# Opening of a two-layer backbone step: small loads on ScalarE's queue, first modulation by halves of the contraction, gate products behind chunk one

## What is computed

```python
sh1, sc1, gt1, sh2, sc2, gt2 = split(silu(cond) @ w_mod[l] + b_mod[l], 6)   # w_mod[l]: 1024 x 6144
h    = rmsnorm(x) * g * (1 + sc1) + sh1              # modulation
proj = h @ w_in                                      # 1024 x 3600: 7 chunks of 512 columns, 16 columns a | b
gate = -exp(a_log) * softplus(proj_a + dt_bias)      # DeltaNet decay, from the last 16 columns
beta = sigmoid(proj_b)
# then: 2-D neighbourhood attention | chunked gated DeltaNet -> w_out -> dense SwiGLU
# layer 1: pooling mixer -> top-2-of-8 SwiGLU experts -> final norm
```

## Time and profile before

| | |
|---|---|
| time before, median of 3 runs | 1436.82 us (1436.22 to 1437.96) |
| the profiled execution | 1437.28 us |
| its span in the profile | 1435.6 us (1.7 us lie around it) |
| PE busy | 1362.7 us, 95% of the span |
| DVE, ACT, POOL busy | 326.4, 306.1, 95.1 us |
| mean DMA rate | 348 GB/s |
| chain that ended last | PE 84%, DMA 7%, SP's issuing side 4%, DVE 3%, ACT 2% |

### The profile page before, as it was taken

One profiled execution on the slowest core, in us unless ns is written; L12 is line 12 of the kernel. 1 busy time (PEld: TensorE's weight loads), 2 busy tenths in 40 slices (PEclk: granted clock), 3 DMA queues, 4 the chain that ended last, 5 costly groups with the idle time before them and its releaser, 6 DMA issues.

```text
span 1435.6 us, 28151 instructions
## 1 busy us (share of the span) xinstructions
PE 1362.7 (95%) x12676; PEld 721.0 (50%) x12676; DVE 326.4 (23%) x415; ACT 306.1 (21%) x404; POOL 95.1 (7%) x175
## 2 busy tenths in 40 slices
PE   4999899889999998999999999999999999999976
PEld 1997586768888875343333333333333343343322
DVE  1564544655444445000000000100000000000005
ACT  2557344443443423010000010010000000010002
POOL 5101040320000001000000000000000000000012
PEclk9799999999999999999999999999999999999999
DMA  8755838899565549999999999999999999999994
GB/s 336 272 180 187 345 155 307 327 391 340 183 197 175 191 173 419 399 424 424 420 424 424 398 425 409 395 422 425 398 424 424 399 423 425 397 419 425 420 422 195
DMA packets 125186, 500.24 MB, mean 348 GB/s; under 512 B 10716, under 2 KB 14632, under 8 KB 103568
## 3 DMA queue, kind: packets, MB, share of 16 engines
q1 hardware_dynamic: 110464, 471.98, 82.7%
q10 hardware_dynamic: 12208, 18.12, 3.5%
q0 software_dynamic: 2400, 8.42, 1.4%
HBM read 478.81 MB, written 19.69 MB: 347 GB/s over the span
## 4 chain that ended last, share of the span: by engine, by line
PE 84%; DMA 7%; SPq 4%; DVE 3%; ACT 2%; issue 1%; ACTq 0%; DVEq 0%
PE ps L2197 34%; PE ps L2245 13%; PE ps L413 6%; PE ps L415 6%; PE ps L414 6%; PE ps L1706 4%; DMA raw<-in_moe_down 4%; PE ps L2240 3%; SPq L536 2%; DMA raw<-in_moe_up 2%; PE ps L1720 2%; PE ps L1811 1%; PE ps L1812 1%; PE ps L1813 1%; DMA raw<-in_w_mod 1%; SPq L433 1%
## 5 line engine op out<-in xcount | busy, mean ns | idle before, releaser
L2197 PE MATMUL ps<-raw,hTf 128*32 128x512 f32 (+1 forms) x2128 | 209.4, 545 | 4.0 <-DMA raw<-in_moe_up 3.2
L2197 PE MATMUL ps<-ring_a,hTf 128*32 128x512 f32 (+1 forms) x2096 | 203.0, 538 | 2.1 <-ACT hTf L1120 1.1
L1658 DVE TENSOR_TENSOR hm<-gate_bc,ps 128x384 f32<-128x384 f32 (+1 forms) x30 | 18.2, 607 | 711.2 <-PE ps L2197 710.3
L376 DVE TENSOR_TENSOR w_lo<-raw,w_hi 128x2048 fp32r<-128x2048 f32 x60 | 138.1, 2308 | 139.8 <-ACT w_hi L372 139.7
L2197 PE MATMUL ps<-ring_b,hTf 128*32 128x384 f32 (+1 forms) x1408 | 139.2, 540 | 4.2 <-DMA ring_b<-in_moe_up 2.9
L372 ACT ACTIVATE w_hi<-raw 128x2048 fp32r<-128x2048 f32 x60 | 114.4, 1913 | 118.9 <-PE ps L415 114.1
L2197 PEld LDWEIGHTS ps<-raw,hTf 128*32 128x32 f32 x2128 | 68.2, 110 | 130.8 <-issue 124.3
L2197 PEld LDWEIGHTS ps<-ring_a,hTf 128*32 128x32 f32 x2096 | 67.9, 110 | 122.2 <-issue 117.8
L413 PE MATMUL ps<-w_hi,hTh 128*128 128x512 f32 x272 | 107.3, 394 | 1.5 <-DVE w_lo L376 1.5
L415 PE MATMUL ps<-w_lo,hTh 128*128 128x512 f32 x272 | 106.6, 392 | 0.0
L414 PE MATMUL ps<-w_hi,hTl 128*128 128x512 f32 x272 | 106.4, 391 | 0.0
(11 more groups left out here) (375 smaller groups left out, 1486.3 us busy)
## 6 DMA issues: line engine op xcount, KB each, us to landing
raw<-in_w_mod SPq DMA_DIRECT2D x48, 1024.0 KB, 7.7
raw<-in_moe_down SPq DMA_DIRECT2D x21, 2048.0 KB, 24.5
ring_a<-in_moe_down SPq DMA_DIRECT2D x21, 2048.0 KB, 25.8
raw<-in_moe_up SPq DMA_DIRECT2D x14, 2048.0 KB, 24.7
ring_b<-in_moe_down SPq DMA_DIRECT2D x14, 2048.0 KB, 24.9
ring_a<-in_moe_gate SPq DMA_DIRECT2D x13, 2048.0 KB, 21.3
raw<-in_moe_gate SPq DMA_DIRECT2D x11, 2048.0 KB, 23.3
ring_a<-in_moe_up SPq DMA_DIRECT2D x10, 2048.0 KB, 19.4
```

Source lines behind the costliest of these rows:

```text
L376: nc.vector.tensor_tensor(w_lo[:, w % SPLIT], raw[:, slot % RAW], w_hi[:, w % SPLIT].bitcast(F32), ALU.subtract).then_inc(s["lo_ready"], 1)
L2197: last = MM(ps[TOK * j:TOK * j + TOK, part % 4, 0:w], hTf1[:, kt, q * P + TOK * g:q * P + TOK * g + TOK], wt[:, kt % 2, j, :], start=kt == ...
```

## The change

SP now issues only `w_mod`, `x` and what follows. The six loads of rows and the four small loads stand at the head of ACT's program, ahead of `csil`, on ACT's own queue. The modulation works by halves of the contraction: `modulate_half(h)` makes the tiles 4h to 4h + 3, DVE for group 0 and ACT for group 1, each half gets its own `hTh` and `hTl`, and chunk one waits for half h of `hTl` only ahead of its own half h. `unit_hi(0)` moves ahead of the modulation on ACT, and `unit_lo(0)` into it on DVE. The gate products (`mix_gates`) move behind chunk one, and the gates' vector work with them. Nothing is computed that was not computed before. "No filler matmuls" in the title of the change says that PE gets no other work in the time in which it waits.

```diff
--- before.py
+++ after.py
@@ -422,21 +422,8 @@
         @block.sync
         def _(sp):
 
-            for part, src in ((rowsA[0:8, :], c_ctx.rearrange("(k p) -> k p", p=P)),
-                              (rowsA[8:16, :], c[0].rearrange("(k p) -> k p", p=P)),
-                              (rowsA[16:48, :], norm_g.rearrange("l w (k p) -> (l w k) p", p=P)),
-                              (rowsA[48:84, :], conv_w[0].rearrange("i (t p) -> (i t) p", p=P)),
-                              (rowsA[84:92, :], pool_scale[0].rearrange("(k p) -> k p", p=P)),
-                              (rowsB[0:96, :], b_mod.rearrange("l (k p) -> (l k) p", p=P))):
-                sp.dma_start(part, src).then_inc(s["rows_loaded"], 16)
             def fetch(dst, src, name):
                 sp.dma_start(dst, src).then_inc(s[name], 16)
-
-            def small_loads():
-                fetch(w_ab[:, :, :], w_in[0].rearrange("(t p) n -> p t n", p=P)[:, :, 7 * 512:7 * 512 + 16], "small_loaded")
-                fetch(alog[:, :], a_log[0].rearrange("d h -> (d h)").partition_broadcast(P), "small_loaded")
-                fetch(dtb[:, :], dt_bias[0].rearrange("d h -> (d h)").partition_broadcast(P), "small_loaded")
-                fetch(ogain[:, :], o_gain[0].partition_broadcast(P), "small_loaded")
 
...
@@ -466,8 +453,6 @@
                 if i == 1:
                     fetch(x[:, 0], x_prompt[0], "x_loaded")
                     fetch(x[:, 1], x_sample[0], "x_loaded")
-                if i == 5:
-                    small_loads()
             for i, (_, ch) in enumerate(WIN_ORDER):
                 if i == 2:
                     cache_loads()
@@ -807,6 +792,18 @@
             def fetch(dst, src, name):
                 act.dma_start(dst, src).then_inc(s[name], 16)
 
+            for part, src in ((rowsA[0:8, :], c_ctx.rearrange("(k p) -> k p", p=P)),
+                              (rowsA[8:16, :], c[0].rearrange("(k p) -> k p", p=P)),
+                              (rowsA[16:48, :], norm_g.rearrange("l w (k p) -> (l w k) p", p=P)),
+                              (rowsA[48:84, :], conv_w[0].rearrange("i (t p) -> (i t) p", p=P)),
+                              (rowsA[84:92, :], pool_scale[0].rearrange("(k p) -> k p", p=P)),
+                              (rowsB[0:96, :], b_mod.rearrange("l (k p) -> (l k) p", p=P))):
+                act.dma_start(part, src).then_inc(s["rows_loaded"], 16)
+            fetch(w_ab[:, :, :], w_in[0].rearrange("(t p) n -> p t n", p=P)[:, :, 7 * 512:7 * 512 + 16], "small_loaded")
+            fetch(alog[:, :], a_log[0].rearrange("d h -> (d h)").partition_broadcast(P), "small_loaded")
+            fetch(dtb[:, :], dt_bias[0].rearrange("d h -> (d h)").partition_broadcast(P), "small_loaded")
+            fetch(ogain[:, :], o_gain[0].partition_broadcast(P), "small_loaded")
+
             act.wait_ge(s["rows_turned"], 1)
             nc.scalar.activation(csil[:, :], ps[:, 7, 0:16], ACT.Silu).then_inc(s["csil_ready"], 1)
 
@@ -848,10 +845,23 @@
                         .then_inc(s["h_hi_ready"], 1)
 
 
+            def modulate_half(h):
+
+                act.wait_ge(s["xn_turned"], 2)
+                for t in range(4 * h, 4 * h + 4):
+                    last = nc.scalar.activation(hTf0[:, t, P:2 * P], ps[:, 6 + h, (t % 4) * P:(t % 4 + 1) * P],
+                                                ACT.Identity, scale=scp[:, 0, t, 1:2], bias=mcol[:, 0, t, 1:2])
+                last.then_inc(s["hT_by_scalar"], 1)
+                act.wait_ge(s["hT_by_scalar"], h + 1)
+                act.wait_ge(s["hT_by_vector"], h + 1)
+                nc.scalar.activation(hTh0[:, 4 * h:4 * h + 4, :], hTf0[:, 4 * h:4 * h + 4, :], ACT.Copy).then_inc(s["h_hi_ready"], 1)
+
             norm(0)
             copy_rows(0, 0)
+            unit_hi(act, 0)
             act.wait_ge(s["scp_ready"], 1)
-            modulate(0, 0, hTf0, hTh0)
+            modulate_half(0)
+            modulate_half(1)
 
 
             def copy_proj(i):
@@ -896,14 +906,13 @@
                 nc.scalar.activation(decay[:, 8 * b:8 * b + 8], decay[:, 8 * b:8 * b + 8], ACT.Exp, scale=-1.0)\
                     .then_inc(s["decay_ready"], 1)
 
-            unit_hi(act, 0)
             unit_hi(act, 1)
             unit_hi(act, 2)
+            unit_hi(act, 3)
+            copy_proj(0)
+            unit_hi(act, 4)
             softplus_in()
-            copy_proj(0)
-            unit_hi(act, 3)
             conv_middle(0)
-            unit_hi(act, 4)
             copy_proj(1)
             unit_hi(act, 5)
             conv_middle(1)
@@ -1266,9 +1275,25 @@
             save_cols(0, 0)
             scales(0, 1)
             dve.sem_inc(s["scp_ready"], 1)
-            modulate(0, 0, hTf0, hTh0, hTl0)
-            dve.wait_ge(s["ab_turned"], 1)
-            nc.vector.tensor_copy(ab.rearrange("p b n -> p (b n)"), ps[:, 2, 0:32]).then_inc(s["cols_saved"], 1)
+            def modulate_half(h):
+
+                dve.wait_ge(s["xn_turned"], 2)
+                for t in range(4 * h, 4 * h + 4):
+                    last = nc.vector.tensor_scalar(hTf0[:, t, 0:P], ps[:, 4 + h, (t % 4) * P:(t % 4 + 1) * P],
+                                                   scp[:, 0, t, 0:1], mcol[:, 0, t, 0:1], ALU.mult, ALU.add)
+                last.then_inc(s["hT_by_vector"], 1)
+
+            def low_half(h):
+
+                dve.wait_ge(s["h_hi_ready"], h + 1)
+                cut = slice(4 * h, 4 * h + 4)
+                VT(hTl0[:, cut, :], hTf0[:, cut, :], hTh0[:, cut, :].bitcast(F32), ALU.subtract).then_inc(s["h_lo_ready"], 1)
+
+            modulate_half(0)
+            unit_lo(dve, 0)
+            low_half(0)
+            modulate_half(1)
+            low_half(1)
             def col(i):
                 return sm[:, i]
 
@@ -1314,14 +1339,14 @@
                 nc.vector.tensor_scalar(decay[:, 8 * b:8 * b + 8], decay[:, 8 * b:8 * b + 8], 0.0, None, ALU.max)\
                     .then_inc(s["diff_ready"], 1)
 
-            unit_lo(dve, 0)
-            unit_lo(dve, 1)
+            for i in range(1, 4):
+                unit_lo(dve, i)
+            dve.wait_ge(s["ab_turned"], 1)
+            nc.vector.tensor_copy(ab.rearrange("p b n -> p (b n)"), ps[:, 2, 0:32]).then_inc(s["cols_saved"], 1)
             gates_in()
-            unit_lo(dve, 2)
+            unit_lo(dve, 4)
             gates_out()
-            unit_lo(dve, 3)
             conv_taps(0)
-            unit_lo(dve, 4)
             unit_lo(dve, 5)
             dve.wait_ge(s["gc_turned"], 1)
             step(nc.vector.tensor_copy(col(10), ps[:, 6, 0:16]))
@@ -1744,14 +1769,15 @@
             turn_cols(0, 0)
 
 
-            pe.wait_ge(s["small_loaded"], 64)
-            pe.wait_ge(s["cols_saved"], 1)
-            for b in range(NB):
-                pe.wait_ge(s["hT_by_scalar"], b + 1)
-                pe.wait_ge(s["hT_by_vector"], b + 1)
-                for t in range(KT):
-                    last = MM(ps[:, 2, 16 * b:16 * b + 16], hTf0[:, t, b * P:b * P + P], w_ab[:, t, :], start=t == 0, stop=t == KT - 1)
-            last.then_inc(s["ab_turned"], 1)
+            def mix_gates():
+
+                pe.wait_ge(s["small_loaded"], 64)
+                pe.wait_ge(s["hT_by_scalar"], 2)
+                pe.wait_ge(s["hT_by_vector"], 2)
+                for b in range(NB):
+                    for t in range(KT):
+                        last = MM(ps[:, 2, 16 * b:16 * b + 16], hTf0[:, t, b * P:b * P + P], w_ab[:, t, :], start=t == 0, stop=t == KT - 1)
+                last.then_inc(s["ab_turned"], 1)
 
             def cumulate():
 
@@ -1789,7 +1815,6 @@
                     last = turn(ps[:, 3, i * P:i * P + P], kTA[:, i, 0:P])
                 last.then_inc(s["k_turned"], 1)
 
-            pe.wait_ge(s["h_lo_ready"], 2)
             pe.wait_ge(s["mod_cols_saved"], 1)
             for i, (kind, _) in enumerate(WIN_ORDER):
                 b0 = 4 * (i % 2)
@@ -1803,6 +1828,8 @@
 
 
                     pe.wait_ge(s["lo_ready"], n + 1)
+                    if i == 0:
+                        pe.wait_ge(s["h_lo_ready"], h + 1)
                     for q in range(4):
                         out = ps[:, b0 + q // 2, (q % 2) * 256:(q % 2 + 1) * 256]
                         for t in range(4):
@@ -1813,6 +1840,8 @@
                             last = MM(out, w_lo[:, n % SPLIT, t, q * P:q * P + P], hTh0[:, kt, :], start=False,
                                       stop=kt == KT - 1 and q % 2 == 1)
                     last.then_inc(s["weights_used"], 1)
+                if i == 0:
+                    mix_gates()
                 if i == 1:
                     cumulate()
                 if i in (2, 3):
```

## The result

The changed kernel took 1434.49 us (median of 20 runs, 1430.45 to 1439.57), the kernel before 1439.06 in the same comparison (20 runs, 1435.65 to 1444.73; the three runs shown ahead of the prediction are among them). The ratio is 0.9973, 95% interval 0.9964 to 0.9983: faster by 0.27%, or 3.9 us (2.4 to 5.2, the ratios times 1439.06). The medians alone differ by 4.6 us. Forecast were 6.5.

What follows compares the result with a forecast made beforehand. Opening bound by `w_mod` loads, with a 3.3 us hole from SP's held `alog` issue, then the chain to chunk one. 4.1 + 5.9 - 3.5 = 6.5 us earlier at chunk two, forecast 1430.5 us, range 1427.2 to 1434.5.

Steps and rivals of the forecast that it cites:

- Term 1: Opening loads: the last `w_mod` product ends 4.1 us earlier, at 28.5 (bounds 2.3 and 5.6), small transfers costing 1.5.
- Term 2: From last `w_mod` product to chunk one: chunk one starts 7.3 us behind it instead of 13.2, saving 5.9 us.
- a `w_hi` that waits long for its load with the modulation behind it: Ahead of chunk one on ACT: listed as a sign that the forecast is wrong; no size given.
- Term 3: Gate products between dense chunks: now on the path, costing 3.5 us at clock 1.00 (bounds 3.5 and 7.0).
- The first: Opening loads: small transfers cost what the hole did; term 1 is 2.3 or less, 1432.5 to 1435; chance 0.13.
- The low clock: At the gate products: clock stays or falls low, 7.0 us instead of 3.5, time 1434; chance 0.06.
- the slower case: Opening: rows come too late behind SP's queued loads, X at 37.8, 2.8 us lost, 1440; chance 0.08.

Runs made afterwards that it cites:

- loads only: Kernel before with the ten small loads (rows, `w_ab`, `alog`, `dtb`, `ogain`) issued on ACT's queue, nothing else changed; ratio to before 0.9978.
- order only: Changed kernel with the ten small loads back on SP in their old places, leaving the halves and the moved gate products; ratio to before 0.9993.
- the small loads behind: Changed kernel with `w_ab`, `alog`, `dtb`, `ogain` issued by SP behind the first two `w_in` units; ratio to before 0.9941, repeated 0.9967.
- spread products: Changed kernel with the gate products in four parts, one behind each quarter of chunk one's second half; ratio to before 0.9979.
- the two broadcasts alone: Changed kernel with only `alog` and `dtb` issued by SP behind the first two `w_in` units; ratio to before 0.9985.
- Four fillers: Changed kernel with four products that nobody reads on PE behind the turned rows, ahead of chunk one; ratio to before 0.9983.
- with six and an earlier chunk one: Changed kernel with four small loads behind two `w_in` units, gate products spread, and six unread products ahead of chunk one; ratio to before 0.9958, median 1431.16 us.

## Why the prediction was right, and where it failed

The time is 4.0 us above the 1430.5 forecast. 2.2 of them are the starting point, three executions of before with a median of 1436.82 where 20 have 1439.06. The rest is the gain, 4.6 us by the medians and 3.9 by the ratio, where 6.5 were forecast.

**Term 1, the last product: right, 4.7 us for 4.1.** SP's hold is gone, the units follow each other, and the small transfers cost 0.9 rather than 1.5 (2.3 + 3.3 - 4.7). Its working on `csil` was off: ACT's issues and table load were forecast to end near 6.8; the issues ended at 9.8 and the load at 11.1, since `alog` and `ogain` held ACT for 2.2 us each. The rows landed at 10.2 instead of 8.3, `csil` ran at 11.14 right behind the table load, and the first product ran at 12.6 instead of 10.4. It cost nothing, as said: five products then run back to back in 7.3 us, and from the sixth (21.30) PE waits for loads again. The Trainium skill (DMA: Bandwidth & Descriptors, Issuing engines are not separate DMA queues) calls the saving of issuing time usually small; here moving the issues alone brought the last product 4.6 us forward (loads only), so this case does not agree.

**Term 2, the step that failed** (a wait that was mis-sized, in a chain that was right): "`w_in` unit 0 lands 2.5 behind `w_mod` unit 7". It landed 4.7 behind (31.44 for 26.72), 3.6 behind the last product instead of 1.4. The chain behind it was right to a tenth: 7.3 in order only, 7.2 with the small loads behind, and 9.4 in the changed kernel, which is 7.3 plus 2.1 to 2.2 of the late unit. I had costed the small transfers against the products alone, in term 1, and at 1 MB in 2.5 us for the unit behind them. They were not through by then, and an alternation of one for one cost the transfer in 2 KB pieces more than `w_mod` with its 8 KB pieces: from 23 to 25.5 us q1 moved 1.03 MB in 142 packets beside 141 of q10, from 25.5 to 28 only 0.51 MB in 256 beside 259. With 0.9 in term 1 and 2.1 here the small transfers cost 3.0 us, not 1.5. The prediction named the sign to look for ("a `w_hi` that waits long for its load with the modulation behind it") but gave it no price. Chunk one took 13.7 us for the 14.0 assumed.

**Term 3, the gate products: right in size, not in what follows.** 3.5 us at clock 1.00 as forecast. That the clock stays there behind them was read from one stretch of one profile. In both profiles of before it does stay there, but in nine of the twelve profiles of the other kernels it falls within those one-column products or at most 1.3 us behind them, and behind the gate products in three of seven. So one stretch of one profile was too little to go by.

**The sum.** 4.7 + 5.9 - 2.1 (late unit) - 3.5 + 0.2 (chunk one, 13.65 for 13.8) = 5.2 us at chunk two (59.58 before, 54.40 now). From there the shift was to be carried one for one, and in the repeat of the changed kernel it nearly was (4.9 at chunk two, 4.6 at the end). The ratio gives 3.9 (2.4 to 5.2), so the 5.2 at chunk two lies at the interval's very edge. In the first profile 3.2 us went in two falls of the clock. A fall behind the gate products, 1.6 us in three of seven profiles, would make 0.7 of the missing 1.3 on the average, an estimate from these rows. Two things speak against resting on it. With spread products the 0.7 should come back, but 0.9979 beside 0.9977 doesn't show it. And over all executions the changed kernel has the higher clock, 0.987 on the mean of its 20, where the kernel before has 0.983 to 0.984 on each of the three chips (21 to 29 executions each). Some of that is the opening, where the low stretch lasts 13.7 us in the profile and lasted 17.1 before. The two profiles of before, 0.987 both, are among its better executions. The clock does go with the time within one kernel: of the 20 runs of the changed kernel, the ten with the lower mean clock (0.9852) average 1436.45 us, the other ten (0.9888) 1433.07. But that the changed kernel loses more to it than the kernel before is not shown, and what takes the 1.3 us stays open. The range was set from terms whose bounds I had, and left this spread out.

**The rivals.** The first came close: the small transfers cost 3.0 us of the 3.3 that it gave them, and the time lies in its band of 1432.5 to 1435. But they cost it on the unit behind the products and not, as the rival had it, on the products. The low clock came behind the gate products, not in them. The rows were late by 2 us and not by 12: one packet for one held, and the slower case never came near. Here too the row decided over the Trainium skill (DMA: Bandwidth & Descriptors, Queues, rings and completion order): 256 packets beside 259 don't look like turns of 9 to 17. Equal sums over 2.5 us could still hide such turns; shorter stretches don't (24 packets beside 23 from 24.0 to 24.5 us, 27 beside 28 in the next half).

**Best version.** The change with the small loads behind the first two `w_in` units, with or without spread gate products: 0.9941, 0.9967 and 0.9945, medians 1429.3 to 1433.5. The traces show the opening 2.6 to 3.4 us shorter than the changed kernel's.

## What to carry to other kernels

When loads are moved to another queue, cost them against every transfer that shares the engines with them, up to the time when the last small piece is through, and above all against the first one that the new order of work wants early. A load of few bytes is no small load where it is hundreds of pieces (`w_ab` is 1024, each broadcast 128): put it behind the last transfer that somebody waits for. Here it took moving all four; the two broadcasts alone gave 0.9 of 2.2 us. And a clock that one profile shows at full speed behind a thin stretch of matmuls is one sample; look at every similar stretch. Here a low stretch of about 1.6 us in cost came in three of seven profiles at one such place, and in nine of fourteen at the other. And look where a profiled execution lies among all: the two of before stood at its better end.

## What the runs showed of the hardware

- Two hardware queues with work shared the engines one packet for one at each size seen here: 142 packets, nearly all of 8 KB, beside 141 of 64 bytes in 2.5 us with the engines busy throughout, and 256 packets of 2 KB beside 259 of some 40 bytes in the next 2.5 us, while the engines are busy for 0.69 of it. Without the broadcasts they are busy for 0.73 of that stretch. Why they stand idle for the rest was not tried.
- The hold at an issue is not SP's own: at `alog`, behind the 1024 runs of `w_ab`, it was 11.44 us on SP before, 5.26 on SP behind the first two `w_in` units, 2.16 on ACT at the start. Nor does it need those runs ahead: with `w_ab` on ACT's queue, SP was held at `alog` for 4.38 us behind the two units, and with all four on SP, `w_ab` itself was held for 3.54. What sets its length was not tried.
- The clock can fall or stay at the same place of the same program: behind the gate products it fell in one execution of the changed kernel and not in the other, with milestones that agree within 0.3 us until then.
- Four fillers (3.6 us at clock 1.00) left a gap of 4.65 us ahead of chunk one and the clock fell in it; with six and an earlier chunk one the gap was 0.66 us and the clock stayed.
